# Square sums moved to GpSimd, the third weight split moved behind the root, and the value evacuation moved to VectorE in a fused two-block transformer kernel

## The reference, cut to what matters

```python
def rms_norm(x, g, eps=NORM_EPS):
    xf = x.astype(jnp.float32)
    y = xf * lax.rsqrt(jnp.mean(xf * xf, axis=-1, keepdims=True) + eps)
    return (y * g.astype(jnp.float32)).astype(x.dtype)

for l in range(2):
    x = x + 0.5 * swiglu(rms_norm(x, ffn_norm[l, 0]), ffn_w_in[l, 0], ffn_w_out[l, 0])
    h = rms_norm(x, mix_norm[l])
    x = x + (rwkv7_time_mix(h, ...) if l == 0 else diff_attention(h, k_sh, v_sh, ...))
    x = x + 0.5 * swiglu(rms_norm(x, ffn_norm[l, 1]), ffn_w_in[l, 1], ffn_w_out[l, 1])
    if l == 0:
        k_sh, v_sh = shared_kv(x, kv_norm, w_kv, k_norm)

# inside rwkv7_time_mix
kk = kk * lax.rsqrt(jnp.maximum(jnp.sum(kk * kk, axis=-1, keepdims=True), 1e-24))   # per head
k = k * (1 + (a - 1) * k_a)
y = wkv7_scan(r, decay, k, v, -kk, kk * a)
```

## Time and profile before

| what | value |
|---|---|
| time, median of 3 runs (range) | 2271.28 us (2264.16 to 2272.87) |
| the profiled execution's own time | 2264.16 us |
| its span in the trace | 2262.4 us |
| PE busy | 2007.3 us (89%) |
| DVE busy | 1342.8 us (59%) |
| ACT busy | 807.4 us (36%) |
| POOL busy | 549.5 us (24%), nearly all of it before 989 us |

### The profile page before, as it was taken

How to read it: one execution, slowest core, us unless ns; L and a number is a source line. 1 busy time by engine, 2 the same in 40 slices (tenths; PEclk the granted TensorE clock), 3 DMA queues, 4 the chain that set the end, 5 groups by cost and what they waited for, 6 DMA issues and landing times.

```text
span 2262.4 us, 37774 instructions
## 1 busy us (share of the span) xinstructions
PE 2007.3 (89%) x15509; PEld 1595.9 (71%) x15509; DVE 1342.8 (59%) x2199; ACT 807.4 (36%) x1207; POOL 549.5 (24%) x573
## 2 busy tenths in 40 slices
PE   5999867877777777779999999999999999969999
PEld 3888853422222222239998789999999999849999
DVE  3456686667667667435557574465566555565554
ACT  2335432222222222224334452253443434454333
POOL 1000067777777777730000000000000000000000
PEclk8999989999999999999999999999999999969999
DMA  9883379999999999975553120135554555403653
GB/s 326 281 271 115 113 286 391 392 385 409 409 404 380 387 409 407 409 264 168 178 189 130 63 76 4 40 131 187 185 181 146 176 184 187 149 20 112 200 173 110
DMA packets 257462, 510.49 MB, mean 226 GB/s; under 512 B 15450, under 2 KB 175900, under 8 KB 254268
## 3 DMA queue, kind: packets, MB, share of 16 engines
q1 hardware_dynamic: 177002, 233.94, 31.3%
q0 software_dynamic: 73728, 268.47, 30.3%
q10 hardware_dynamic: 6610, 6.36, 1.0%
HBM read 507.68 MB, written 1.05 MB: 225 GB/s over the span
## 4 chain that ended last, share of the span: by engine, by line
PE 61%; POOL 19%; issue 7%; DVE 5%; DMA 4%; ACT 3%; ACTq 0%; SPq 0%; DVEq 0%
PE bank L621 21%; POOL big L1487 19%; PE bank L382 13%; PE bank L636 11%; PE bank L1928 4%; PE bank L351 3%; DMA big<-in_peer_v,aux 2%; PE bank L1398 2%; DMA big<-in_w_mod 2%; PE bank L876 1%; DVE w_lo L301 1%; PE bank L557 1%; PE bank L1781 0%; DVE big L1578 0%; ACT w_hi L297 0%
## 5 line engine op out<-in xcount | busy, mean ns | idle before, releaser
L1398 PE MATMUL bank<-big 128*128 128x512 f32 x1024 | 505.6, 619 | 166.9 <-DMA big<-in_peer_v,aux 151.3
L301 DVE TENSOR_TENSOR w_lo<-w_raw,w_hi 128x2048 fp32r<-128x2048 f32 x198 | 453.4, 2291 | 323.5 <-ACT w_hi L297 323.5
L1398 PEld LDWEIGHTS bank<-big 128*128 128x128 f32 x1024 | 176.0, 190 | 491.6 <-DMA big<-in_peer_v,aux 344.3
L297 ACT ACTIVATE w_hi<-w_raw 128x2048 fp32r<-128x2048 f32 x198 | 377.0, 1905 | 210.3 <-PE bank L621 81.0
L1578 DVE SCALAR_TENSOR_TENSOR big<-big,aux 128x1024 f32<-128x1024 f32 x256 | 313.6, 1225 | 219.1 <-DMA big<-in_peer_u,aux 218.4
L621 PE MATMUL bank<-hh,w_hi 128*128 128x256 f32 x1344 | 380.9, 283 | 0.0
L621 PE MATMUL bank<-hh,w_lo 128*128 128x256 f32 x1344 | 380.3, 283 | 0.0
L621 PE MATMUL bank<-hl,w_hi 128*128 128x256 f32 x1344 | 380.3, 283 | 0.0
L1487 POOL DMA_INDIRECT big<-in_peer_u,aux x256 | 270.0, 1055 | 105.1 <-issue 76.6
L1487 POOL DMA_INDIRECT big<-in_peer_v,aux x256 | 259.1, 1012 | 88.9 <-issue 69.7
L1472 ACT ACTIVATE big<-ident,aux 128x128 f32<-128x128 f32 x256 | 101.7, 400 | 441.8 <-PE bank L1398 346.1
(11 more groups left out here) (388 smaller groups left out, 2838.2 us busy)
## 6 DMA issues: line engine op xcount, KB each, us to landing
w_raw<-in_ffn_w_in SPq DMA_DIRECT2D x88, 1024.0 KB, 5.1
w_raw<-in_ffn_w_out SPq DMA_DIRECT2D x44, 1024.0 KB, 4.9
big<-in_w_mod SPq DMA_DIRECT2D x24, 1024.0 KB, 5.0
w_raw<-in_w_in SPq DMA_DIRECT2D x22, 1024.0 KB, 7.7
w_raw<-in_rwkv_w_rkv SPq DMA_DIRECT2D x12, 1024.0 KB, 5.0
w_raw<-in_peer_w_query SPq DMA_DIRECT2D x8, 1024.0 KB, 5.3
w_raw<-in_w_kv SPq DMA_DIRECT2D x8, 1024.0 KB, 5.3
w_raw<-in_w_out SPq DMA_DIRECT2D x4, 1024.0 KB, 5.3
```

Source lines behind the costliest of these rows:

```text
L297: act.activation(w_hi[i][:, :], w_raw[i][:, :], ACT.Copy).then_inc(S("w_hi"), 1)
L301: dve.tensor_tensor(w_lo[i][:, :], w_raw[i][:, :], w_hi[i][:, :].bitcast(F32), ALU.subtract)\
L1398: mm = pe.matmul(bank[4 + 2 * tt + half][:, :], diag[:, turn % RROWS, :], ring_rows[turn % RROWS][:, half * 512:(half + 1) * 512], start=( ...
```

## The change

1. The squares of the five norms and their sum over the eight feature tiles are made by GpSimd (`squares_pool`: four products and three additions of 128x512, strictly one after the other, each piece behind its own `xf_ready`). ACT's squares go. PE's sum is two products instead of eight.
2. In an FFN, PE's square sum stands behind slot base+1 instead of behind slot base. ACT splits slot base+2 behind the root instead of ahead of it, and DVE splits it behind the inverse.
3. In RWKV, the rounding of v's input to `hh` (four pieces, ahead of the read-out of k's last product) becomes one instruction behind that read-out, and PE starts RKV+8 only when `hh` and `hl` are whole.
4. In RWKV, ACT's root of the head sums stands behind the exponentials and a split instead of ahead of them; the four `values_out` move from ACT to DVE.
5. In diff, the gains stand ahead of the exponential of lambda on ACT instead of behind it.

```diff
         def gain_hi(act, n, hh_free):
-            def square(kp):
-                if n in SUMS:
-                    act.activation(mix_squares[:, 2 * kp:2 * kp + 2, :], xf[:, 2 * kp:2 * kp + 2, :], ACT.Square)\
-                       .then_inc(S("mix_squares"), 1)
             act.wait_ge(S("slot_done"), hh_free)
-            for kp in range(2):
-                gain(kp)
-                square(kp)
...
-            if n in SUMS:
-                load_root(act)
+            for k in range(KT):
+                if k % 2 == 0:
+                    xf_piece(act, n, k // 2)
+                act.activation(hh[:, k, :], xf[:, k, :], ACT.Copy, scale=col(GAIN[n], k)).then_inc(S("gain_hi"), 1)
...
+        def squares_pool(pool, n):
+            o = pool_order[0]
+            for kp in range(4):
+                xf_piece(pool, n, kp)
+                part = xf[:, 2 * kp:2 * kp + 2, :].rearrange("p k t -> p (k t)")
+                if kp == 0:
+                    o(pool.tensor_tensor(square_sum, part, part, ALU.mult))
+                    continue
+                o(pool.tensor_tensor(square_new, part, part, ALU.mult))
+                o.wait()
+                o(pool.tensor_tensor(square_sum, square_sum, square_new, ALU.add))
+                o.wait()
+            pool.sem_inc(S("square_sum"), 1)
+
         def square_sum_pe(pe, n):
-            for k in range(KT):
-                if k % 2 == 0:
-                    pe.wait_ge(S("mix_squares"), 4 * ROOTS.index(n) + k // 2 + 1)
-                mm = pe.matmul(bank[3][:, 0:T], ones[:, 0:P], mix_squares[:, k, :], start=(k == 0), stop=(k == KT - 1))
+            pe.wait_ge(S("square_sum"), ROOTS.index(n) + 1)
+            for half in range(2):
+                mm = pe.matmul(bank[3][:, 0:T], ones[:, 0:P], square_sum[:, half * T:(half + 1) * T],
+                               start=(half == 0), stop=(half == 1))
...
             up(base, 0, base % WRING, bank[0], None, fresh_norm(pe, norm))
+            up(base + 1, 0, (base + 1) % WRING, bank[1], None)
             if norm in SUMS:
                 square_sum_pe(pe, norm)
-            up(base + 1, 0, (base + 1) % WRING, bank[1], None)
...
             gain_hi(act, norm, base)
-            hi.upto(base + 2)
+            hi.upto(base + 1)
             if norm in SUMS:
+                load_root(act)
                 rms_root(act, norm)
...
+            hi.upto(base + 2)
             silu(0, base)
...
             gain_lo(dve, norm)
-            lo.upto(base + 2)
+            lo.upto(base + 1)
             if norm in SUMS:
                 rms_inverse(dve, norm)
...
+            lo.upto(base + 2)
             gate(0, base, bank[0])
...
+            pe.wait_ge(S("act_split"), SPLITS["mix_v"])
             for j in range(4):
-                project(pe, RKV + 8 + j, hh, hl, "F", fresh(pe, "mix_hi", 5, 2, "mix_v") if j == 0 else None)
+                project(pe, RKV + 8 + j, hh, hl, "F")
...
             for j in range(4):
                 hi.upto(RKV + 4 + j + 2)
-                if j == 3:
-                    act.wait_ge(S("mixed"), 5)
-                    act.wait_ge(S("slot_done"), RKV + 8)
-                    for kp in range(4):
-                        act.activation(hh[:, 2 * kp:2 * kp + 2, :], mixed[1][:, 2 * kp:2 * kp + 2, :], ACT.Copy)\
-                           .then_inc(S("mix_hi"), 1)
...
+            mix_hi(2, 6)
             hi.upto(RKV + 10)
...
             a.then_inc(S("key_factor"), 1)
-            head_root_act(act, 0)
...
-            def values_out(j):
-                b, free = evac_ready(act, RKV + 8 + j)
-                act.activation(vT[:, 2 * j:2 * j + 2, :], b[:, :], ACT.Copy).then_inc(free, 1)
             hi.upto(RKV + 11)
-            values_out(0)
-            hi.upto(RKV + 12)
-            values_out(1)
+            head_root_act(act, 0)
             hi.upto(RKV + 13)
-            values_out(2)
-            values_out(3)
...
-            split_rest(dve, mixed[1], "mix_hi", 5)
+            rest(2, 6)
             lo.upto(RKV + 10)
-            head_guard_dve(dve, 0, 1e-24, None, ALU.max, ALU.bypass)
+            def values_out(j):
+                b, free = evac_ready(dve, RKV + 8 + j)
+                dve.tensor_copy(vT[:, 2 * j:2 * j + 2, :], b[:, :]).then_inc(free, 1)
+
             dve.wait_ge(S("key_factor"), 1)
             o(dve.tensor_tensor(keyT, keyT, scratch, ALU.mult))
+            head_guard_dve(dve, 0, 1e-24, None, ALU.max, ALU.bypass)
+            o.wait()
+            values_out(0)
             head_inverse_dve(dve, 0)
...
+            gain_hi(act, 7, DQ - 2)
             act.wait_ge(S("lam_dve"), 1)
             act.activation(lam_exp, lam_exp, ACT.Exp).then_inc(S("lam_exp"), 1)
-            gain_hi(act, 7, DQ - 2)
+            load_root(act)
```

29 lines of the change are left out of this document (16 added, 13 removed).

## The result

The changed kernel takes 2298.67 us (median of 4 runs, 2296.36 to 2298.92) against 2271.61 us of the kernel before, run on the same chip: slower by 27 us. Those four are not all: 21 executions of the changed kernel are on record, from 2294.65 to 2311.14 us, 2302.4 on average, and the ratio on record is 1.0141, 95% interval 1.0112 to 1.0170, which is 32 us. I had forecast 2286.5 us, 15.2 more than before: the direction and the range held, but the loss is about twice what I forecast. The profiled execution took 2309.7 us, in a span of 2308.0 us.

What follows compares the result with a forecast made beforehand. From 1000 us on, almost unbroken TensorE work was taken to bound the kernel. FFNs +10.0, KV -2.3, diff -4.7 and RWKV +12.2 sum to +15.2 us; scaled to the median, 2286.5 us, range 2274 to 2302 us.

Steps and rivals of the forecast that it cites:

- 1, fewer products: TensorE's square sum in five places: two products instead of eight, saving 2.59 us in each.
- 2, squares off ScalarE: Openings of FFN 1 and 3: TensorE no longer waits for gains queued behind squares, saving 0.75 us each.
- 3, the FFN wait: FFN 0, 1 and 3: TensorE waits 4.67 us ahead of the third slot, plus 1.74 us for the lower clock.
- 4, KV: KV's opening: 2.59 us of products saved, 0.3 us charged for a tie with GpSimd's sum; -2.3 us.
- Rival A: GpSimd's squares collide with VectorE's two-input SBUF operations, GpSimd some 5 us late in diff; +12 us, 2298 us, chance 0.25.
- 5, diff: Diff's opening: gains first remove TensorE's idle of 2.64 us, and the first read-out comes earlier; -4.7 us.
- 6, RWKV: RWKV ahead of the scan: VectorE's inverse waits for the late root, delaying the turning of v; +12.2 us.
- B: RWKV: TensorE's v products, not VectorE, set the scan's start, up to 3 us earlier; total 2271 us, chance 0.10.
- C: The clock holds in all waits and RWKV comes at its lower value; +7 us, 2278 us, chance 0.18.

Runs made afterwards that it cites:

- e2: Kernel before with GpSimd's squares and the two-product sum in all five places, sum still behind one slot; 2312.92 us, ratio 0.9975.
- e8: Kernel before with GpSimd's squares and two-product sum in the three FFNs alone, and diff's gains ahead of the exponential; 2305.02 us, ratio 0.9939.
- e5: Changed kernel with GpSimd writing constants in place of the squares and their sums, reading nothing; 2337.50 us once, kernel before 2319.0 on that chip.
- e3: Kernel before with the FFN order alone (sum behind two slots, third slot's split behind the root), ScalarE's squares and eight products kept; 2337.74 us, ratio 1.0094.
- e6: Changed kernel with RWKV's head root ahead of the exponentials again; 2351.18 us once, kernel before 2319.0 on that chip.
- e9: Changed kernel with v rounded ahead of k's last read-out again, in four pieces; 2315.41 us once, kernel before 2267.16 on that chip.
- e11: Changed kernel with GpSimd's squares held back until VectorE's gains of that norm are done; 2301.52 us once, kernel before 2267.16 on that chip.
- e10: Changed kernel with the FFNs' third slot's split ahead of root and inverse, sum left behind two slots; 2283.26 us once, kernel before 2267.16 on that chip.
- e4: Kernel before with diff's gains ahead of lambda's exponential on ScalarE alone, root table loaded behind that exponential; 2310.97 us, ratio 0.9976.
- e7: Kernel before with v's four read-outs moved to VectorE, root and rounding left in place; 2327.65 us once, kernel before 2319.0 on that chip.

## Why the prediction was right in direction and wrong in size

- **1, fewer products, -2.59 us each: right.** e2 and e8 show 2.43 to 2.58 us per FFN.
- **2, squares off ScalarE, -0.75 us in FFN 1 and 3: wrong.** The time between the gains on ScalarE went, and the collision on VectorE took its place: FFN 1's first slot takes 6.58 us (1529.93 to 1536.51), where it took 6.51. It takes 5.99 us in e5, where nothing collides, so there was 0.5 us to win and not 0.75. Missed: 1.5 us in FFN 1 and 3 together.
- **3, the FFN wait: right in mechanism and in the wait (4.67 forecast, 4.76 measured), mis-sized in the clock.** The two slots behind the wait take 13.86 us from start to start in FFN 1 (13.73 and 14.15 in FFN 0 and 3) instead of 11.52: 2.2 to 2.6 us, not 1.74. I had taken the price of an idle of 2.64 us for one of 4.76 (and that one is 1.57 when the slot, 7.33 us, is counted from start to start as well). The granted clock read 0.50 and 0.75 in the two stretches behind the wait, 8 us; in the earlier trace rows it was 0.57 over 4 us. The price isn't fixed either: behind the same 4.76 us of wait the two slots took 13.07 to 14.31 us in e3, e5, e6, e9 and e11, 1.6 to 2.8 us more, so my 1.74 lies at the low end of what occurs. Missed over three FFNs: about 2.0 us for the clock, and 0.7 for the sum and the wait together, which took 5.79 us each where I had 0.87 + 4.67.
- **4, KV, -2.3 us: the step that failed.** The size of GpSimd's instructions was right: 1.04 to 1.10 us a square and 1.26 to 1.35 a sum, against 1.26 estimated, and the sum is ready ahead of TensorE. That is in part because TensorE itself is late: the sum is done 7.52 us behind the down products (1736.48 - 1728.96), 1.8 us later than an unhindered first slot ends, where I had called it a tie. But I asked only whether GpSimd would be late and charged nothing for what it does to VectorE. The measured +6.26 us: first slot +5.36 (3.99 us of waits for `hl`, the rest low clock), from there to the head sum -0.65 (the products saved, less about 1.9 us of low clock), and from the head sum on +1.55, the second fall of the clock, which e5 has without the collision and e10 lacks with it. Missed: 8.6 us, over half of the whole miss; 7 of it are the collision and the clock right behind it, 1.55 a fall whose cause stays open. Rival A named the collision. That its total, 2298 us, is the median of four is luck: its terms (KV from -2.3 to +3, diff from -4.7 to -1, two FFNs by 1) add to 11 us and not to 12, and its working had the wrong victim: it let GpSimd be 5 us late for the sum, and charged the FFNs as its neighbours 1 us each. Measured is a GpSimd 1.8 us late, hidden behind a VectorE 4.6 us late. The argument I held against A, gathers of 1055 ns beside VectorE's work, had already been marked as not deciding; I should have given A more than 0.25. The Trainium skill ("SBUF — State Buffer", section "SBUF: two separate sides") has it as an exclusive lock, held for the whole instruction, between a VectorE operation with two SBUF inputs and a GpSimd one that reads SBUF. The trace agrees: 3.02 us for a square beside a split, and 485 ns at most for the gains where GpSimd reads nothing.
- **5, diff, -4.7 us: the idle went as forecast, and the collision put another in its place.** e4 alone gives 3.2 us, short of 4.7 by less than diff scatters, and e5 and e8, also without the collision in diff, took 116.27 and 116.10 us; the whole change gives 1.6, which is within the scatter, with TensorE's idle gone from the start of the slot and back inside it, where TensorE waits 3.93 us for `hl`:

```profile
1993.01 3.66 PE L352 MATMUL bank<-hl,w_hi 128*128 128x256 f32 x16 [3.93 <-DVE hl L535]
```

- **6, RWKV, +12.2 us: right in size (+12.5), half right in the reason.** The inverse starts 21.5 us behind the last k product (some 21 forecast, 13.25 before), the turning of v 10.7 us late behind it (49.86 against 39.19 us; 9.4 us late when counted from FFN 0's end), and it takes 5.42 us instead of 3.75, the 1.7 us that I had added for the clock. The remaining 1.5 us are in the scan, within its scatter. But I put all on the root behind the exponentials. The late rounding makes TensorE's head sum late by itself and would have been enough; e6 and e9 show that undoing either alone gains nothing, e7 that undoing both gains 5 us. The wait ahead of the inverse is split into 5.66 us for TensorE and 1.60 us for ScalarE. That the size came out with half of the reason is luck.
- **Rivals.** A held, with the victim exchanged. B fell with e7. C fell: the clock did not hold behind the FFN waits.

The sum of the misses is 4.3 us in the FFNs, 8.6 in KV, 3.1 in diff and 0.3 in RWKV: 16.3 us, which is 31.5 less 15.2. Of the FFNs' 4.3, 1.5 is part 2, about 2.0 the clock and 0.7 the sum and the wait.

## What to carry to other kernels

Work moved to an idle GpSimd isn't free because it ends in time: ask what VectorE does meanwhile, and whether someone waits for that; if so, and if VectorE's operations have two SBUF inputs, price GpSimd's reading instructions as if they stood in VectorE's own queue. A sum that a later split or activation stands behind belongs as early as its inputs allow, since every queue behind it then has slack. And before a step is called the cause of a delay, undo the others as well: two late steps can each hold the same third one, and undoing one alone shows nothing. A price that hangs on TensorE's clock wants several executions: the same wait cost 1.6 to 2.8 us behind it.

## What the runs showed of the hardware

- VectorE and GpSimd take turns by whole instructions when GpSimd reads SBUF and VectorE's operation has two SBUF inputs: eight such operations took 7.82 us instead of 3.25, five of them held by one GpSimd instruction each; a GpSimd square took 3.02 us instead of 1.04 beside a split of 2.28. A GpSimd that only writes costs VectorE nothing (3.25 us), and a VectorE operation with one input in PSUM isn't held (0.68 us beside a square).
- The turns go both ways. VectorE's split took 2.94 us instead of 2.28 behind a GpSimd square that had begun 0.25 us before it (e11_later).
- TensorE's low clock behind an idle of 4.76 us cost 2.2 to 2.6 us in the two slots behind it in the changed kernel, and 1.6 to 2.8 us over five others; after an idle of 2.21 us in e10_split it cost nothing (granted clock 1.00).
- The clock falls in the same code in one execution and not in another: at KV's head products it read 0.66 and 0.50 in the changed kernel and 1.00 in e10_split, 3 us of KV's time.
